# Two fixed experts as first units, shared down products beside units, and row transposes on VectorE in a mixture-of-experts decoder layer

## The reference

```python
s = sigmoid(x @ w_router)                      # 544 x 64 experts
# group-limited top 8 of 64, weights wsel = s / sum(s) * 2.5
def expert(acc, xs):                           # 64 experts, FF = 256
    wg, wu, wd, ge = xs
    y = (silu(x @ wg) * (x @ wu)) @ wd
    return acc + ge[:, None] * y, None
shared = (silu(x @ ws_gate) * (x @ ws_up)) @ ws_down
x = layernorm(ALPHA * x + gt2 * (routed + shared))
```

## Time and profile before

| what | us |
|---|---|
| median of 3 runs (1498.76 to 1503.31) | 1503.09 |
| the profiled execution | 1499.84 |
| its span | 1498.1 |
| TensorE busy | 1373.6 |
| VectorE busy | 565.4 |
| ScalarE busy | 291.3 |
| GpSimd busy | 313.3 |

### The profile page before, as it was taken

The page is one execution under the profiler, slowest core; times in us unless marked ns, Lnnn a source line. Parts: engine busy times, 40 slices in busy tenths (PEclk is TensorE's granted clock), DMA queues, the critical chain, the costliest instruction groups (busy, mean ns, idle before and its releaser), DMA issues. The chain is left out here.

```text
span 1498.1 us, 21979 instructions
## 1 busy us (share of the span) xinstructions
PE 1373.6 (92%) x8512; PEld 790.1 (53%) x8512; DVE 565.4 (38%) x1292; ACT 291.3 (19%) x674; POOL 313.3 (21%) x334
## 2 busy tenths in 40 slices
PE   5999999999979999889999799999899999999966
PEld 3775777764657776767454333434343444434322
DVE  2101455453632674435887343211111111212138
ACT  1002333354223222111121001111111111111021
POOL 6000000000059995100045111111111111111000
PEclk9999999999989999989999899999999999999988
DMA  9510410123464442684203999999999999999685
GB/s 338 177 56 26 125 58 1 57 86 113 135 186 140 133 149 87 192 312 149 81 29 96 393 384 421 420 419 405 410 394 406 408 407 412 393 403 392 235 316 228
DMA packets 106805, 358.52 MB, mean 239 GB/s; under 512 B 28837, under 2 KB 31013, under 8 KB 80581
## 3 DMA queue, kind: packets, MB, share of 16 engines
q1 hardware_dynamic: 81288, 301.98, 52.5%
q0 software_dynamic: 15968, 40.61, 7.4%
q10 hardware_dynamic: 9446, 14.51, 2.8%
HBM read 331.49 MB, written 38.15 MB: 247 GB/s over the span
## 5 line engine op out<-in xcount | busy, mean ns | idle before, releaser
L2152 PE MATMUL bank<-arena 128*32 128x512 f32 (+2 forms) x1536 | 331.4, 610 | 20.6 <-DMA arena<-in_w_up 20.3
L2152 PEld LDWEIGHTS bank<-arena 128*32 128x32 f32 (+2 forms) x1536 | 119.3, 137 | 202.0 <-issue 201.2
L2160 PE MATMUL bank<-arena 128*32 128x512 f32 (+2 forms) x768 | 168.1, 597 | 0.9 <-DVE arena L2930 0.9
L2139 POOL DMA_INDIRECT expert_rows<-arena x46 | 46.4, 1008 | 483.4 <-PE bank L2145 384.1
L2924 DVE TENSOR_TENSOR arena<-arena,bank 128x256 f32<-128x256 f32 x46 | 19.4, 421 | 318.6 <-ACT arena L2572 318.6
L1226 PE MATMUL bank<-arena 128*128 128x272 f32 x512 | 131.3, 410 | 8.0 <-DMA arena<-in_w_in 7.4
L454 PE MATMUL bank<-arena 128*128 128x272 f32 x480 | 112.9, 398 | 4.5 <-DVE arena L2014 2.1
L1226 PEld LDWEIGHTS bank<-arena 128*128 128x128 f32 x512 | 97.6, 196 | 34.6 <-issue 12.8
L2160 PEld LDWEIGHTS bank<-arena 128*32 128x32 f32 (+2 forms) x768 | 56.5, 134 | 106.0 <-issue 104.8
L454 PEld LDWEIGHTS bank<-arena 128*128 128x128 f32 x480 | 92.3, 193 | 24.6 <-issue 2.8
L684 PE MATMUL bank<-arena 128*128 128x272 f32 x384 | 99.7, 403 | 0.0
(11 more groups left out here) (485 smaller groups left out, 1787.1 us busy)
## 6 DMA issues: line engine op xcount, KB each, us to landing
arena<-in_w_gate SPq DMA_DIRECT2D x64, 1024.0 KB, 12.9
arena<-in_w_up SPq DMA_DIRECT2D x64, 1024.0 KB, 17.6
arena<-in_w_down SPq DMA_DIRECT2D x64, 1024.0 KB, 16.2
arena<-in_w_ada SPq DMA_DIRECT2D x12, 2048.0 KB, 9.0
arena<-in_w_in SPq DMA_DIRECT2D x11, 2048.0 KB, 10.3
arena<-expert_rows SPq DMA_DIRECT2D x8, 2048.0 KB, 25.4
gate_logits<-arena ACTq DMA_DIRECT2D x16, 272.0 KB, 3.5
arena<-gate_logits SPq DMA_DIRECT2D x8, 544.0 KB, 5.0
```

Of the source, the lines that this page charges most:

```text
L2139: return nc.gpsimd.indirect_dma_start(out=y_d, out_offset=bass.IndirectOffsetOnAxis(ap=rows, axis=0), in_=of, in_offset=None, bounds_check ...
L2152: mm = nc.tensor.matmul(out[rows].rearrange("p (a n) -> p a n", a=2), x[:, k, rows], gate_up_slot(n)[:, :, k, :], start=k == 0, stop=k == ...
L2160: mm = nc.tensor.matmul(out[rows, :], h[:, k, rows], down_slot(n)[:, k, 512 * half:512 * half + 512], start=k == 0, stop=k == 1)
```

## The change

- Experts 0 and 1 are taken out of the ranking (sorted last) and become units 0 and 1, of one load each. Their weights are issued by number, without the order. Their row lists are made on the chip: a one-hot of each token's place in the list (`first_one_hots`), a matmul with the token values (`first_rows`), five VectorE steps (`first_indices`). Their rows are gathered by GpSimd into the result buffers, before `lists_in`.
- There are now 47 units: 2 fixed, then 45 from `spread` with 5 instead of 6 units of kind N (TNTTXPNWW...), 64 loads as before.
- `unit_rows` on TensorE and `unit_indices` on VectorE move behind the gate and up product and `hidden` of unit 0. Down of load 4 waits for them (before it was gate of load 4).
- All five shared down products stand beside units 2, 3, 4, 5 and 8. None stands ahead of unit 0.
- The rows are turned by VectorE: 16 transposes of 32x256 a unit, each of eight 32x32 blocks. The 8 TensorE transposes and both copies go.
- Gathers go 5 units ahead instead of 3. Units 0 to 10 use two result buffers instead of four.
- `gate_sums` and `gate_values` move from units 1 to 6 to units 6 and 10 to 14.

```diff
-for kind in spread(dict(X=8, W=12, T=12, N=6), 3, 0):
+for i in range(NF):
+    LOADS.append(None)
+    UNITS.append((LISTED + i, segments(P, (i, P))))
+for kind in spread(dict(X=8, W=12, T=12, N=NPAIR), 3, 0):
...
-            if name == "w_down" and n == 0 and dn is dl[0]:
-                sp.wait_ge(lists_in.sem, 16)
+            if name == "w_down" and n == 4 and dn is dl[4]:
+                sp.wait_ge(tab_out.sem, 32)
+                sp.wait_ge(unit_done.sem, 1)
...
-    BESIDE = (2, 3, 4)
+    BESIDE = {2: 0, 3: 1, 4: 2, 5: 3, 8: 4}
+    Y_OF = [u % 2 if u < max(BESIDE) + 3 else u % RY for u in range(NU)]
...
             load_shared(ws[1], "ws_down")
+            for n, e in enumerate(FIXED):
+                load_expert(sp, n, e, gl[n], dl[n])
             sp.wait_ge(order_done.sem, 1)
             ord_out.inc(sp.dma_start(order_d.rearrange("e o -> o e"), order_row), 16)
             sp.wait_ge(ord_out.sem, 16)
-            load_by_rank(sp, 0)
-            load_by_rank(sp, 1)
             load_by_rank(sp, 2)
             sp.wait_ge(su_mm.sem, NT)
-            load_by_rank(sp, 3)
-            sp.wait_ge(tab_out.sem, 32)
-            sp.wait_ge(unit_done.sem, 1)
-            for n in range(4, E):
+            for n in range(3, E):
                 load_by_rank(sp, n)
...
+            def first_rows():                              # TensorE, after overflow_sums
+                pe.wait_ge(first_made.sem, NT)
+                for i in range(NF):
+                    for t in range(NT):
+                        mm = nc.tensor.matmul(bank[4][:, 256 + i:257 + i], first_hot[t][i][0:TOKS[t]], first_val[i][0:TOKS[t], t:t + 1],
+                                              start=t == 0, stop=t == PT)
+                first_mm.inc(mm)
...
             up(4)
-            unit_rows()
-            down(0)
-            down(1)
...
             for u in range(NU):                            # TensorE
                 if u:
                     hiddenT(u - 1)
-                if u + 1 < NU:
-                    xT(u + 1)
-                if 1 <= u <= len(BESIDE):
+                if u - 1 in BESIDE:
                     shared_step("high", BESIDE[u - 1])
                 gate_up_of(u)
+                if u == 0:
+                    unit_rows()
+                    pe.wait_ge(s_hid.sem, NT)
...
+                if t == 0:                                 # GpSimd, behind the entries of tile 0
+                    pool.wait_ge(wo_mm.sem, 2 * NT)
+                    places_made.inc(pool.iota(places, ...))
...
+            def first_one_hots(t):                         # VectorE; t = 0, 1, 2 ahead of choose(3), 3 and 4 behind order_and_excess
+                step(TT(place_in[0:n, t, :], key[0:n, t, 0:NF], ebase[0:n, 0:NF], ALU.subtract))
+                step(TT(first_val[1][0:n, t:t + 1], first_val[1][0:n, t:t + 1], selm[0:n, t, 0:1], ALU.subtract))
+                for i in range(NF):
+                    ins = TS(first_hot[t][i][0:n], places[0:n], place_in[0:n, t, i:i + 1], None, ALU.is_equal)
...
+            def xT(u):                                     # VectorE
+                if u >= 2:
+                    dve.wait_ge(gu_mm.sem, u - 1)
+                for a in range(4):
+                    slots = slice(QUAD * a, QUAD * a + QUAD)
+                    by_quarter = row_buffer(u)[slots].rearrange("p (k q j) -> p q k j", k=KD, q=4)
+                    for q in range(4):
+                        ins = nc.vector.transpose(XT[u % 2][QUAD * q:QUAD * q + QUAD, :, slots], by_quarter[:, q])
+                ins.then_inc(xt_v.sem, 1)
...
+            shared_hidden(4)
+            overflow_table()
+            xT(0)
+            dve.wait_ge(xt_v.sem, 1)
+            copy_lists()
             for u in range(NU):                            # VectorE
                 if u:
                     hiddenT(u - 1)
-                if u + 1 < NU:
-                    xT_high(u + 1)
-                if 1 <= u <= len(BESIDE):
+                if u - 1 in BESIDE:
                     fold_beside(1, BESIDE[u - 1])
+                if u >= 2 and u + 1 < NU:
+                    xT(u + 1)
                 hidden(u)
+                if u == 0:
+                    unit_indices()
+                    xT(1)
                 if u:
                     y_high(u - 1)
+                if u == 1:
+                    xT(2)
```

More of the change, by code:

```diff
@@ L75, in spread @@
     return order
-heavy, wide, three, pairs = iter(range(HEAVY)), iter(range(HEAVY, THREE)), iter(range(THREE, WIDE)), iter(range(PAIRED, PAIRED + 6))
-for kind in spread(dict(X=8, W=12, T=12, N=6), 3, 0):
+heavy, wide, three, pairs = iter(range(HEAVY)), iter(range(HEAVY, THREE)), iter(range(THREE, WIDE)), iter(range(PAIRED, LISTED))
+for i in range(NF):
+    LOADS.append(None)
+    UNITS.append((LISTED + i, segments(P, (i, P))))
+for kind in spread(dict(X=8, W=12, T=12, N=NPAIR), 3, 0):
     n = len(LOADS)
@@ L2101, in build @@
     TAIL = [PT, 0, 1, 2, 3]
+    first_hot = [[at(T1 + 1024 + P * (NF * t + i), P) if t < PT else at(T2 + 1024 + P * i, P) for i in range(NF)] for t in range(NT)]
+    places, place_in = at(T2 + 1280, P), at(T2 + 1408, NT, NF)
+    first_val = [at(T2 + 1408 + NF * NT + NT * i, NT) for i in range(NF)]
+    assert T2 + 1408 + 2 * NF * NT <= WS0 and NF * PT * P <= 1024
+    row_buffer = lambda u: Yb[u] if u < NF else Xg[(u - NF) % RX]
     rows_s = at(T2 + 2 * D, 2, D)
@@ L2283, in up @@
                     su_mm.inc(mm)
[L2285 to L2305, removed]
             def counts():
@@ L2367, in _ @@
             overflow_sums()
+            first_rows()
             up(3)
@@ L2391, in shared_step @@
                 sd_mm.inc(mm) if half else sd_low.inc(mm)
[L2393 to L2398, removed]
             def gate_up_of(u):
                 parts = UNITS[u][1]
-                pe.wait_ge(xt_a.sem, u + 1)
                 pe.wait_ge(xt_v.sem, u + 1)
@@ L2654, in scatter @@
                 col = UNITS[u][0]
-                scatter_rows(to_rows[:, col:col + 1], Yb[u % RY]).then_inc(y_out[u % RY].sem, 16)
-            pool.wait_ge(h2_store.sem, 16 * NT)
+                scatter_rows(to_rows[:, col:col + 1], Yb[Y_OF[u]]).then_inc(y_out[Y_OF[u]].sem, 16)
             pool.wait_ge(unit_done.sem, 1)
             pool.wait_ge(su_mm.sem, PT)
-            for u in range(RX - 1):
+            for u in range(NF, NF + RX):
                 gather(u)
-            for u in range(NU):
-                if u + RX - 1 < NU:
-                    gather(u + RX - 1)
-                if u:
-                    scatter(u - 1)
+            for u in range(1, NU):
+                if u + NF + RX - 1 < NU:
+                    gather(u + NF + RX - 1)
+                scatter(u - 1)
             scatter(NU - 1)
             for j in range(RY):
-                pool.wait_ge(y_out[j].sem, 16 * len(range(j, NU, RY)))
+                pool.wait_ge(y_out[j].sem, 16 * Y_OF.count(j))
             def late(i):
@@ L2776, in shared_hidden @@
                 s_hid.inc(TT(h, h, up, ALU.mult))
-            def shared_fold(t):
-                n = TOKS[t]
-                dve.wait_ge(sd_mm.sem, t + 1)
-                for half in range(2):
-                    cols = slice(512 * half, 512 * half + 512)
-                    x = x_tm[0:n, t, cols]
-                    step(TT(shD[0:n], bank[DOWN_BANKS[t][half]][0:n, :], gt2b[0:n, t // PT, cols], ALU.mult))
-                    ins = STT(x, x, ALPHA, shD[0:n], ALU.mult, ALU.add)
-                    done(s_fold, ins) if half else step(ins)
             def totals():
@@ L2793, in rank_experts @@
                 step(STT(keyf, base[0:E], float(E), ids, ALU.mult, ALU.subtract))
+                step(TS(keyf[:, 0:NF], keyf[:, 0:NF], -LAST, None, ALU.add))
                 dve.wait_ge(cnt_mm.sem, 1)
                 count = bank[7][0:E, 256:257]
-                step(STT(keyp, count, float(E), e, ALU.mult, ALU.subtract))
+                step(STT(keyp, count, float(E), sort_id[0:E], ALU.mult, ALU.subtract))
                 step(nc.vector.tensor_copy(nsort[:, 1:2], count))
@@ L2898, in _ @@
             overflow_rows()
-            copy_lists()
-            overflow_table()
             shared_hidden(3)
-            unit_indices()
-            shared_hidden(4)
-            shared_fold(0)
             def fold_beside(half, t):
                 n = TOKS[t]
-                dve.wait_ge(sd_mm.sem, t + 1) if half else dve.wait_ge(sd_low.sem, t - 1)
+                dve.wait_ge(sd_mm.sem, t + 1) if half else dve.wait_ge(sd_low.sem, t + 1)
                 cols = slice(512 * half, 512 * half + 512)
```

139 lines of the change are left out of this document (80 added, 59 removed).

## The result

| | before | after |
|---|---|---|
| median, us | 1502.38 | 1575.35 (1571.55 to 1584.18, 4 runs) |
| profiled execution | 1499.84 | 1575.79 |
| its span | 1498.1 | 1574.1 |
| ratio, 95% interval | | 1.0499 [1.0451, 1.0546] |

The changed kernel is 5% slower: 73 us by the medians, 76 between the two profiled executions, where 5 us of gain were forecast. The range (to 1514) doesn't hold the time, and the slowest rival (VectorE as the bound, 1538) is still 37 us short of it.

The account below looks back on a forecast made before the run. Taken as bound: the DMA flow, 9.19 us a load against 8.8 at full flow, TensorE close behind. Last product 1402.5 against 1408.0, so -5.5 us on 1499.8 gives 1494.3, 1498 as median; range 1483 to 1514.

Parts of the forecast that it names:

- What follows is unchanged.: After the last gate and up product, forecast at 1402.5 against 1408.03: the rest of the kernel takes as long as before.
- 50 x 8.8 = 440.: Loads after load 13: 50 loads at 8.8 us each take 440 us, where the kernel before takes 459.5.
- Unit 8 at 957.5 plus 5: Gate and up of load 13 land at 957.5; 5 us are added for TensorE still some 10 us behind the weights.
- the flow is nearly full again from 906.5: Units 3 to 5: each takes 17 us of TensorE, two loads with rows 17.6, so weights flow nearly fully.
- The start: Up to load 13: first product at 836.9, 6.2 us won, then chained transposes leave the change 9 us behind.
- The order's store at 810, load 2 at 813: At the start: the order store moves from 807.05 to 810, and load 2 is issued at 813.
- Transposes at 0.43, held by the quarters, free in the loop: VectorE: sixteen transposes without overlap take 6.9 us a unit; 8.4 us of VectorE work fits under 10.85.
- The flow does not rise: Rival for the later loads: 9.19 us a load belongs to the transfers, the start's 9 us stay, 1512; chance 0.20.
- TensorE was the bound: Rival for the units: the 45 us taken off TensorE count, 31 less at unit 46, 1472; chance 0.11.
- VectorE becomes the bound: Rival for the units: at 0.69 us a transpose a unit takes 12.5 us, 1538; chance 0.09.
- Start and flow cancel: Rival: 1 us more in each chained step at the start, or 8.9 us a load, gives 1503; chance 0.16.

Follow-up runs that it names:

- b_mix: The changed kernel with one unit of kind T replaced by one of kind N, so that every expert fits its units; 1529.79 us, ratio 1.014.
- j_late3: The kernel before with the first place's capacity entered as 100 rows instead of 192, which makes one late unit certain; 1554.38 us, ratio 1.0338.
- i_half_up: b_mix with half of each gate and up product left out, all weights still loaded; 1506.58 us, measured once.
- d_pe_turn: b_mix with the rows of all 47 units transposed on TensorE again; 1509.13 us, ratio 0.9989.
- g_order: d_pe_turn with the order of the experts stored from ScalarE's queue instead of SyncE's; 1506.85 us, ratio 1.003.
- n_split: d_pe_turn with only units 0 to 2 turned on TensorE and those from unit 3 on turned on VectorE; 1502.53 us, ratio 0.9985.
- p_no_gather2: i_half_up with the gathers left out as well, all but row 0; 1465.77 us, measured once.

## Why the prediction was wrong

By its own steps:

- *"What follows is unchanged."* The first failed step, and the largest: 49 us (after), 54 (b_mix), 51 (j_late3). The prediction counted "64 loads" and never asked whether the 62 ranked experts still fit their places when SMALL goes from 52 to 50. It would have needed the counts of rows by expert, which no profile shows; but the mechanism stood in the code, a loop of 36 turns that is skipped as long as nothing overflows, its price could have been bounded (the load, gather and product of one unit with nothing beside them), and it should have been a rival.
- *"50 x 8.8 = 440."* The second: 50 loads after load 13 took 1434.36 - 977.01 = 457.4, 9.15 each, 17 us more. A stretch of 10 us at 422 GB/s was taken for a flow that lasts. At i_half_up's pace of 9.07 us a load, with a quarter less of TensorE's work, 50 loads would gain 5 to 6 us over before, not 20.
- *Unit 8 at 957.5 plus 5.* It started at 977.01, 14.5 later. Nearly all of it is the weights: those of load 13 land at 971.1 (up issued at 953.79, 17.3 us to land) and not at 957.5. Product 2, 7.5 us late (884.19 and not 876.7), is half of that. The rest is *"the flow is nearly full again from 906.5"*: from 906 to 920 it is 206 GB/s, and 417 only from 920 on. TensorE's lag, put at 5 us, is 5.9.
- These add up: 14.5 + 17.4 + 49.3 = 81.2, against 1574.1 - (1498.1 - 5.5) = 81.5.
- *The start.* The mechanism was right: a chain over products 0, 1, 2, 20 us apart (20.0 and 21.1 measured; forecast 19.4 and 20.4), low clock after each pause, loads 4 to 6 bound to it. The first product came at 843.02 and not 836.9: 2.5 us are this execution's earlier stages (`ws_down` at 795.92 instead of 793.44), the one-hots took 3.7 for 3, `first_rows` 2.65 for 2, TensorE waited 1.2 for VectorE ahead of the last shared up product, and xT(0) took 7.2 for 6.9; 0.8 is left over. The cost of it, though, was said to be 9 us at load 13; by b_mix against d_pe_turn it is 20.7 at the end.
- *The order's store at 810, load 2 at 813.* Store 813.92, load 2 826.34. The prediction did note that loads 0 and 1 move ahead, but not that the store stands behind their 6 MB. By g_order this costs nothing in time.
- *Transposes at 0.43, held by the quarters, free in the loop.* Right: 435 ns, 16 in 7.18 us, and n_split shows the 44 later ones at no cost in time. `hidden` does wait some 0.4 us on them, where the prediction had it covered, and TensorE doesn't feel it. The Trainium skill, "VectorE: DVE Perf Modes", section "Two Vector instructions with no wait between them", says that a change of output quadrant holds the next instruction; 16 x 0.435 = 6.96 in 7.18 agrees, with no overlap between them.
- *The rivals.* "The flow does not rise" (1512) was right in its mechanism. With 20.7 us at the start instead of 9 it gives 1524, and b_mix measured 1.014, 1524 on before's 1503. That is no second proof, since the 20.7 come from b_mix; what shows it is the flow. "TensorE was the bound" fell with i_half_up: 93 us less of TensorE's work from 880 to 1370 than in b_mix (446 to 353) moved the pace from 9.10 to 9.07 us a load. "VectorE becomes the bound" fell too: in after it is busy 358 of 490 us, and after product 2 TensorE waits for it about 9 us in all (3.2 for `hidden`, 6.2 for the folds of the shared products). "Start and flow cancel" (1503) needed 8.8 or 8.9 a load, and after ran at 9.15.

## What to carry to other kernels

Before costing a change that regroups work by size, ask what the overflow path costs and whether it is still empty: here one expert in a serial fallback outweighed everything else, and a third of its price was the empty rest of the loop. Take the ceiling of a flow from a long stretch, not from its best 10 us. An operation that is free in a steady loop isn't free in the chain that starts the loop; move it only where there is cover, as n_split does.

## What the runs showed of the hardware

- A 32x256 transpose of four-byte data on VectorE takes 435 ns, and 16 of them over four quarters 7.18 us (after).
- A 256-byte store to HBM, issued behind 6 MB of weights in the same queue, is readable after 11.3 us (after); from another queue after 6.7 (g_order); with nothing ahead of it after 1.1 (before).
- Weights in 1 MB loads with 4 KB rows beside them flow at 408 to 409 GB/s over 320 us, with TensorE busy 218 us of them (i_half_up) or 294 (after). Without the gathers 415 (p_no_gather2, once).
- A product after 8 to 9 us of idle takes 9.4 to 10.2 us instead of 7.1. In after the first such product runs 5 us at a granted clock of 0.50 (1.2 GHz) and then at 1.00. The three at the start of b_mix are 8.6 us of the 20.7. Over 490 us the mean granted clock was 0.97 in after (448 us busy) and 0.87 in i_half_up (353).
- An empty turn of the fallback loop takes 0.43 us, 35 of them 15 us.
